# Layer one's running modulation parts: from TensorE rows to VectorE sums and TensorE columns

## The reference

```
mod   = silu(c)     @ w_mod[l] + b_mod[l]     # (6*1024); split into sh1, sc1, gt1, sh2, sc2, gt2
mod_c = silu(c_ctx) @ w_mod[l] + b_mod[l]
h = modulate(rms_norm(x, g_norm1[l]), sh1, sc1)
...                                            # attention, differential attention, convolution, merge
x = x + gt1 * y
h = modulate(rms_norm(x, g_norm2[l]), sh2, sc2)
x = x + gt2 * ((silu(h @ w_g) * (h @ w_u)) @ w_ffn_out)
```

## Time and profile before

| | |
|---|---|
| median of 3 runs | 2515.21 us (2509.43 to 2518.45) |
| span of the profiled execution | 2511.4 us, 34741 instructions |
| time of the profiled execution beyond its span | not shown apart; the median is 3.8 us above the span |
| PE busy, PEld busy | 2411.4 us (96%), 2171.6 us (86%) |
| DVE, ACT, POOL busy | 1223.0 us (49%), 1114.2 us (44%), 999.6 us (40%) |
| DMA | 209.07 MB, mean 83 GB/s |
| mean granted TensorE clock | 0.988 of 2.4 GHz |

### The profile page before, as it was taken

The page is one execution under the profiler, slowest core; times in us unless marked ns, Lnnn a source line. Parts: engine busy times, 40 slices in busy tenths (PEclk is TensorE's granted clock), DMA queues, the critical chain, the costliest instruction groups (busy, mean ns, idle before and its releaser), DMA issues.

```text
span 2511.4 us, 34741 instructions
## 1 busy us (share of the span) xinstructions
PE 2411.4 (96%) x13568; PEld 2171.6 (86%) x13568; DVE 1223.0 (49%) x1901; ACT 1114.2 (44%) x2219; POOL 999.6 (40%) x771
## 2 busy tenths in 40 slices
PE   7999999999989989999999998998999999999999
PEld 4888999889989989999999997777777877788887
DVE  5666677799943331111111126767878973311111
ACT  4666666542253253323322336656664253422222
POOL 2211122176555435555554542111224655444443
PEclk9999999999999999999999999999999999999999
DMA  6100111032223323333333322011112224233333
GB/s 247 43 26 26 34 43 43 18 103 86 75 94 118 121 65 112 118 107 112 114 107 98 118 71 89 26 43 34 43 40 70 93 87 137 81 99 99 95 97 96
DMA packets 117393, 209.07 MB, mean 83 GB/s; under 512 B 13680, under 2 KB 30320, under 8 KB 117104
## 3 DMA queue, kind: packets, MB, share of 16 engines
q1 hardware_dynamic: 117232, 206.86, 25.8%
HBM read 202.62 MB, written 4.19 MB: 82 GB/s over the span
## 4 chain that ended last, share of the span: by engine, by line
PE 51%; DVE 9%; ACT 3%; issue 2%; POOL 0%; DVEq 0%; ACTq 0%
PE acc L577 15%; PE acc L579 14%; PE acc L578 14%; DVE X L1674 4%; PE sco L699 2%; DVE RB L1551 1%; DVE M L1551 1%; ACT M L1006 1%; PE sco L749 1%; PE aux L762 1%; PE aux L577 1%; PE aux L578 1%; PE aux L579 1%; DVE NM L1594 1%; ACT RB L1006 1%
## 5 line engine op out<-in xcount | busy, mean ns | idle before, releaser
L499 POOL TENSOR_TENSOR WLO<-STG,WHI 128x512 fp32r<-128x512 f32 (+2 forms) x760 | 995.6, 1337 | 1493.4 <-ACT WHI L1002 1493.0
L577 PE MATMUL acc<-H,WHI 128*128 128x384 f32 (+2 forms) x1976 | 714.3, 361 | 19.7 <-DVE H L1780 12.1
L578 PE MATMUL acc<-H,WHI 128*128 128x384 f32 (+2 forms) x1976 | 696.4, 352 | 0.0
L579 PE MATMUL acc<-H,WLO 128*128 128x384 f32 (+2 forms) x1976 | 696.4, 352 | 0.0
L1002 ACT ACTIVATE WHI<-STG 128x512 fp32r<-128x512 f32 (+2 forms) x760 | 409.8, 591 | 488.9 <-PE acc L579 433.2
L577 PEld LDWEIGHTS acc<-H,WHI 128*128 128x128 f32 x1976 | 375.4, 190 | 49.2 <-issue 19.6
L579 PEld LDWEIGHTS acc<-H,WLO 128*128 128x128 f32 x1976 | 374.4, 189 | 25.7
L578 PEld LDWEIGHTS acc<-H,WHI 128*128 128x128 f32 x1976 | 375.6, 190 | 24.2
L1674 DVE SCALAR_TENSOR_TENSOR X<-U,WDW,X 128x783 f32<-128x783 f32 (+1 forms) x248 | 298.1, 1251 | 5.0 <-ACT X L1006 3.3
L577 PE MATMUL acc<-RB,WHI 128*128 128x384 f32 (+1 forms) x816 | 289.6, 355 | 5.8 <-DVE M L1551 5.4
L579 PE MATMUL acc<-RB,WLO 128*128 128x384 f32 (+1 forms) x816 | 287.7, 353 | 0.0
(11 more groups left out here) (134 smaller groups left out, 2924.8 us busy)
## 6 DMA issues: line engine op xcount, KB each, us to landing
STG<-in_w_fi SPq DMA_DIRECT2D x176, 256.0 KB, 2.9
STG<-in_w_mod SPq DMA_DIRECT2D x160, 256.0 KB, 2.7
STG<-in_w_in SPq DMA_DIRECT2D x104, 256.0 KB, 2.7
STG<-in_w_gate SPq DMA_DIRECT2D x96, 256.0 KB, 2.6
STG<-in_w_fo SPq DMA_DIRECT2D x64, 256.0 KB, 2.8
STG<-in_w_br SPq DMA_DIRECT2D x96, 128.0 KB, 2.1
FIRST<-in_w_mod SPq DMA_DIRECT2D x8, 1024.0 KB, 20.0
STG<-in_w_out SPq DMA_DIRECT2D x32, 256.0 KB, 2.9
```

The source lines that it names most:

```text
L499: nc.gpsimd.tensor_tensor(WLO[:, s, a:a + w], STG[:, g, a:a + w], WHI[:, s, a:a + w].bitcast(F32), ALU.subtract).then_inc(S("w_split"), 1)
L577: nc.tensor.matmul(dst, lh, rh, start=first, stop=False)
L578: nc.tensor.matmul(dst, lh, rl, start=False, stop=False)
L579: return nc.tensor.matmul(dst, ll, rh, start=False, stop=last)
```

## The change

The 56 mod tiles of layer 0's feed-forward leave the common list, and with them their `hi()`, `split`, `mod_half`, `mod_row`, `turn_mod` and `mod_group`. In their place:

- SP loads the same weights as 56 raw tiles of 512 KB (`raw`), 1 KB runs, into three slots of `M`: two after each up stage (none at stage 0 of group 0), one after each of the first 8 and 6 down tiles of groups 0 and 1. From the fourth on, each waits until DVE has used the raw tile three before.
- DVE weighs each raw tile (`weigh_raw`) after the stage's other work, in two instructions: for the first three parts both streams, 128 x 1024 each; for the last four the latent stream alone, in two halves of 128 x 512. Each adds to an accumulator `GV` in `M` or `U`.
- When eight raw tiles (one part) are in, PE sums over partitions (`turn_cols`): for each chunk of 128 channels and each stream one matmul with `GV` as the stationary operand and one column of ones as the moving one; 16 or 8 float32 matmuls, straight into columns of `sco`. DVE adds the bias (`col_sum`). Four parts are turned in the feed-forward, three around the norm between the layers.
- `U` is cleared on POOL after the third tile of layer 1, not on DVE in the merge of layer 0. The silu of c has a tile of its own, the context half of layer 1's `MOD` is cleared at the start, and PE's wait for the middle chunks stays at the first down tile only.

```diff
+LATER = [(0, GT2), (1, SH1), (1, SC1), (1, GT1), (1, SH2), (1, SC2), (1, GT2)]
+STREAMS = [2, 2, 2, 1, 1, 1, 1]
+RAWS = len(LATER) * KC
+RAW_UP = [[0, 2, 2, 2, 2, 2, 2, 2], [2] * 8, [2] * 6]
+RAW_DOWN = [[1] * 8, [1] * 6 + [0, 0], [0] * 8]
+TURN_UP = {(0, 6): 0, (1, 2): 2, (1, 6): 3}
+TURN_DOWN = {(0, 4): 1}
+RAW_SLOTS = 3
...
+        RAW = [M[:, D * i:D * (i + 1)] for i in range(RAW_SLOTS)]
+        GV = [[t[:, o + D * i:o + D * (i + 1)] for i in range(n)]
+              for (t, o), n in zip(((M, 3 * D), (U, 0), (M, 3 * D), (M, 5 * D), (U, 0), (U, D), (U, 2 * D)), STREAMS)]
...
+            def raw(i):
+                n, k = divmod(i, KC)
+                l, part = LATER[n]
+                g = l * MOD_GROUPS + part * 4
+                if i < RAW_SLOTS:
+                    sp.wait_ge(S("h_ready"), 2 * KC)
+                else:
+                    sp.wait_ge(S("gv"), 2 * (i - RAW_SLOTS + 1))
+                src = w_mod[g:g + 4, k // 4, :, k % 4 * MOD_GROUP:(k % 4 + 1) * MOD_GROUP].rearrange("g p c -> p g c")
+                sp.dma_start(RAW[i % RAW_SLOTS].rearrange("p (g c) -> p g c", g=4), src).then_inc(S(f"raw{i % RAW_SLOTS}"), 16)
...
                 for g, (k0, n) in enumerate(GROUPS):
                     for f in range(n):
                         for s in range(2):
-                            if mod_here(l, g, f):
-                                tile(w_mod[mods // 2, s], KC * P)
-                                mods += 1
                             tile(w_fi[l, f * 2 + (2 * k0 + s)], KC * P)
+                        for i in raws(l, "up", g, f):
+                            raw(i)
                     for j in range(KC):
-                        if mod_out(l, g, j):
-                            tile(w_mod[mods // 2, j % 2], KC * P)
-                            mods += 1
                         tile(w_fo[l, j][:, k0 * P:(k0 + n) * P], n * P)
+                        for i in raws(l, "down", g, j):
+                            raw(i)
...
+                    if l and t == 2:
+                        pool.wait_ge(S("col_full"), len(LATER))
+                        nc.gpsimd.memset(U[:, :], 0.0).then_inc(S("u_zero"), 1)
...
+            def turn_cols(n):
+                pe.wait_ge(S("gv"), 2 * KC * (n + 1))
+                if n >= 4:
+                    pe.wait_ge(S("col_sum"), n - 3)
+                for k in range(KC):
+                    for s in range(STREAMS[n]):
+                        mm = nc.tensor.matmul(turned_cols(n)[:, k, s:s + 1], GV[n][s][:, k * P:(k + 1) * P], ONES[:, 0:1],
+                                              start=True, stop=True)
+                mm.then_inc(S("col_full"), 1)
...
                 if l:
+                    turn_cols(4)
                     norm(l, 0, TOK)
+                    turn_cols(5)
+                    turn_cols(6)
...
+                        if l == 0 and (g, f) in TURN_UP:
+                            if g == 0:
+                                pe.wait_ge(S("mod_sum"), 1 + c.at("turn"))
+                            turn_cols(TURN_UP[g, f])
                         for s in range(2):
-                            if mod_here(l, g, f):
-                                mod_half(s)
-                            tile(KC, normed, slim, between=turn_pending if s == 0 else None)
+                            tile(KC, normed, slim)
...
+            def weigh_raw(i):
+                n, k = divmod(i, KC)
+                dve.wait_ge(S(f"raw{i % RAW_SLOTS}"), 16 * (i // RAW_SLOTS) + 16)
+                if k == 0 and n in (2, 4):
+                    dve.wait_ge(S("col_full"), n - 1 if n == 2 else 2)
+                w = RAW[i % RAW_SLOTS]
+                for u in range(2):
+                    if STREAMS[n] == 2:
+                        src, dst, gain = w, GV[n][u], SC[:, k, u:u + 1]
+                    else:
+                        src, dst, gain = w[:, 512 * u:512 * (u + 1)], GV[n][0][:, 512 * u:512 * (u + 1)], SC[:, k, 0:1]
+                    if k == 0:
+                        nc.vector.tensor_scalar(dst, src, gain, None, ALU.mult).then_inc(S("gv"), 1)
+                    else:
+                        dve.wait_ge(S("gv"), 2 * (i - 1) + u + 1)
+                        nc.vector.scalar_tensor_tensor(dst, src, gain, dst, ALU.mult, ALU.add).then_inc(S("gv"), 1)
...
-                if l == 0:
-                    dve.wait_ge(S("c_split"), CC * (l + 1))
-                    nc.vector.memset(U[:, :], 0.0).then_inc(S("u_zero"), 1)
...
+                        for i in raws(l, "up", g, f):
+                            weigh_raw(i)
+                        if l == 0 and (g, f) in TURN_UP:
+                            col_sum(TURN_UP[g, f])
```

More of the change, by code:

```diff
@@ L160, in weight_tiles @@
         for g, (_, n) in enumerate(GROUPS):
-            w += [KC * P] * ((4 * n - 2 * (g == 0)) if l == 0 else 2 * n)
-            for j in range(KC):
-                w += ([KC * P] if mod_out(l, g, j) else []) + [n * P]
+            w += [KC * P] * (2 * n) + [n * P] * KC
     return w
@@ L322, in qk_count, with raws, turned_cols @@
             return 13 * l + (2 + j if j < 4 else 5 + 2 * (j - 3))
-        def mod_here(l, g, f):
-            return l == 0 and (g or f) > 0
+        def raws(l, counts, g, i):
+            order = [(a, b) for a in range(len(GROUPS)) for b in [("up", f) for f in range(GROUPS[a][1])] + [("down", j) for j in range(KC)]]
+            table = {"up": RAW_UP, "down": RAW_DOWN}
+            done = sum(table[kind][a][b] for a, (kind, b) in order[:order.index((g, (counts, i)))])
+            return range(done, done + table[counts][g][i]) if l == 0 else range(0)
+        def turned_cols(n):
+            o = 512 * (n // 2 % 2)
+            return sco[n % 2][:, o:o + 2 * KC].rearrange("p (k s) -> p k s", s=2)
         def paired(l, j):
@@ L511, in _ @@
             for l in range(DEPTH):
-                for _ in range(26):
+                for t in range(26):
                     split(KC * P)
+                    if l and t == 2:
+                        pool.wait_ge(S("col_full"), len(LATER))
+                        nc.gpsimd.memset(U[:, :], 0.0).then_inc(S("u_zero"), 1)
                 for kind, _, _ in merge_order(l):
@@ L951, in _ @@
                             tile_pair(slim, slim, 2 * KC * l + KC, (l, "up", 0), (l, "up", 1))
-                            at["turned", l, "up", g, f] = c.at("turn")
                             continue
+                        if l == 0 and (g, f) in TURN_UP:
+                            if g == 0:
+                                pe.wait_ge(S("mod_sum"), 1 + c.at("turn"))
+                            turn_cols(TURN_UP[g, f])
                         for s in range(2):
-                            if mod_here(l, g, f):
-                                mod_half(s)
-                            tile(KC, normed, slim, between=turn_pending if s == 0 else None)
-                        at["turned", l, "up", g, f] = c.at("turn")
-                    if g == len(GROUPS) - 1:
-                        turn_pending()
-                    for j in range(KC):
[L962 to L966, removed]
+                            tile(KC, normed, slim)
+                    for j in range(KC):
+                        if l == 0 and (g, j) in TURN_DOWN:
+                            turn_cols(TURN_DOWN[g, j])
+                        tile(m, mid, slim, ready=("mid_chunks", 1 + FC * l + k0) if j == 0 else None)
         @block.scalar
@@ L1524, in _ @@
                         hi()
[L1525 to L1528, removed]
+                        if squares and j == 1:
+                            act.wait_ge(S("gv"), 2 * RAWS)
+                            act.wait_ge(S("col_full"), 4)
                         if squares and j:
@@ L1889, in _ @@
                 norm(l, 0, TOK)
+                if l:
+                    for i in (4, 5, 6):
+                        col_sum(i)
                 if l == 0:
@@ L2032, in _ @@
                             c.step(name)
+                        for i in raws(l, "up", g, f):
+                            weigh_raw(i)
+                        if l == 0 and (g, f) in TURN_UP:
+                            col_sum(TURN_UP[g, f])
+                    if g == 0:
+                        dve.wait_ge(S("col_sum"), 7 if l else 1)
                     for j in range(KC):
-                        mod_groups(at["turned", l, "down", g, j])
+                        if l == 0 and (g, j) in TURN_DOWN:
+                            col_sum(TURN_DOWN[g, j])
                         residual(l, j, slim, GT2)
+                        for i in raws(l, "down", g, j):
+                            weigh_raw(i)
                         if j and l < DEPTH - 1 and g == len(GROUPS) - 1:
```

33 lines of the change are left out of this document (14 added, 19 removed).

## The result

The median is 2522.11 us (2511.57 to 2527.94, 20 runs) against 2512.68 us of the kernel before (2508.11 to 2519.50, 20 runs). The ratio is 1.0031 with a 95% interval of 1.0021 to 1.0041: slower, by some 8 us, where the forecast was 2497.4 us. The profiled execution is one of the faster: it took 2516.45 us, with a span of 2514.6, at a granted clock of 0.982, while the median clock of the 20 runs is 0.979 (0.988 in the profiled execution of before).

The account below looks back on a forecast made before the run. PE, busy for 96% of the span, was taken to bound the kernel. The terms -64.1 - 1.3 + 14.6 + 28 + 5 = -17.8 us, from 2515.2, gave 2497.4 us, with a range of 2483 to 2509.

Parts of the forecast that it names:

- 28 groups leave PE: Layer 0's feed-forward: 28 groups of two modulation tiles and one turn, 2.29 us each, leave PE: 64.1 us less.
- wait behind the first pair: PE's 1.75 us wait behind the first pair, for POOL's split of the fourth tile, mostly goes: 1.3 us less.
- four turns: Feed-forward: 112 one-column load-and-matmul pairs at 0.12 us, plus 0.3 for entering and leaving each call: 14.6 us more.
- fifteen waits: PE waits at up stages for an accumulator held by late loads, 5 of 2.6 and 10 of 1.55 us: 28 more.
- half clock: Lower PE clock behind the five waits of 2.6 us, 0.6 of them dropping it: 5 us more (0 to 25).
- The late raw load: Up stages: raw load waits for DVE, delaying the product tile and ACT's Silu; accumulator free 10.9 us after PE's previous-stage end.
- the eighteen stages: Raw tile late at stages 2 to 7 of group 0, 1 to 7 of group 1, 1 to 5 of group 2.
- Its size: SP's queue: raw tile and both product halves, 1 MB, take 5.4 us to the last half, making PE wait 2.6 us.
- The clock: Behind PE's waits: a drop costs 1.7 us, 0.6 of five long waits drop, none behind 1.5 us: 5 us more.
- The late loads drop the clock: Rival, up stages: last half 0.8 us later, fifteen waits grow by 12 us, clock falls each time: 2530 us, chance 0.15.
- The loads are in time: Rival, up stages: the next product tile lands before about 7.3 us, nothing waits, -50.8 us: 2464 us, chance 0.15.
- POOL and DVE: Rival: POOL and DVE block each other at each first weighing, 15 x 1.04 = 15.6 us: 2513 us, chance 0.12.

Follow-up runs that it names:

- e7: The kernel of e1 with each turn of the feed-forward cut in two, four chunks before one tile and four before the next: 2465.9 us, ratio 0.9801.
- e9: The change with the turns before up stages (0,7), (1,3) and (1,7) in place of (0,6), (1,2) and (1,6): 2518.9 us, ratio 1.0013.
- e11: The change, with SP issuing an up stage's second product tile (from stage 2 on) only when ACT has rounded the first: 2501.8 us, ratio 0.9942.
- e3: The change with only half of each raw tile loaded, 256 KB in place of 512: 2512.5 us, ratio 0.9993.
- e5: The change with every weighing 512 columns wide, the other 512 channels left out for the first three parts: 2504.4 us, ratio 0.9954.
- e10: The change, its late loads included, with each turn of the feed-forward cut in two: 2515.4 us, ratio 1.0010.
- e1: The change with SP's second raw load of an up stage moved behind the next product tile: 2469.0 us, ratio 0.9808.
- e2: The change with ACT doing both Silus before both roundings in layer 0's up stages, SP's order kept: 2467.1 us, ratio 0.9807.
- e4: The kernel of e1 with the four column sums (turns) of the feed-forward made twice: 2491.2 us, ratio 0.9902.

## Why the prediction failed, by its own steps

| term | forecast, us | profiled execution, us |
|---|---|---|
| 28 groups leave PE | -64.1 | -64.1 |
| wait behind the first pair | -1.3 | -1.4 |
| four turns | +14.6 | +12.2 |
| fifteen waits | +28 | +38.0 |
| half clock | +5 | about +14.8 |
| leaving and entering at the waits | nothing | about +4.0 |
| sum | -17.8 | +3.5 (measured +3.1) |

The last two terms together are PE's busy time for the same instructions, 583.36 us after less 564.52 in e7, 18.8 us. The feed-forward of e7 has no half rate but that behind its first pair:

```profile
895.40:1462.60 567.20, 564.52 (x3280) 564.23 (x3281) 249.96 (x296) 142.37 (x256) 213.32 (x136) 0.99 0.35 114
```

The stretches at half rate are 29.7 us long in the change, so they cost 14.8. The other 4 us are the ends of the fifteen waits, some 0.27 us each: the last matmul ahead of a wait overlaps with none behind it (0.16), and the first step behind it is 0.28 us in place of 0.17, as here, where the clock did not fall:

```profile
942.59 0.44 PE L600 MATMUL acc<-H,WHI 128*128 128x384 f32 x1 [2.06 <-ACT G L1042]
942.88 0.34 PE L601 MATMUL acc<-H,WHI 128*128 128x384 f32 x1
943.05 0.34 PE L602 MATMUL acc<-H,WLO 128*128 128x384 f32 x1
```

- **What leaves PE: right.** From the first product (897.73) to turn 4 (1462.67), e7's feed-forward takes 564.9 us, 53.8 less than before. -64.1 - 1.4 + 12.0 for its turns is -53.5. That the 2.29 us of a group came from one step of the chain was enough.
- **The turns: right in kind, 2.4 us too dear.** 0.109 us a pair, next to the dense row of 0.116; entering and leaving is in it. That they are hidden between the layers held.
- **The late raw load: right in place, chain and number.** SP's wait on DVE, the eighteen stages, the three hidden by turns (e9), none in the down part, the weighing's 1.22 us from start to start against 1.28. In the stage shown, PE went on at 1006.20, 11.05 us behind t = 0 (995.15, 0.10 before DVE's T at 995.25); forecast 10.9.
- **Its size: one of the two steps that failed, 10 us.** "The raw tile and both halves are 1 MB: 3.3 + 2.1 = 5.4 us to the last half." It counted what is ahead of the last half in SP's list and not what SP, once let go, issues right behind it: 2 MB in 2.4 us. At (0,4) the raw load went out behind 974.70 + 2.44 = 977.1, and ACT could round the second half at 983.92 only, 6.8 us later (DVE, then ACT):

```profile
974.70 4.87 DVE L1797 SCALAR_TENSOR_TENSOR M<-M,SC 128x1024 f32<-128x1024 f32 x4
```

```profile
982.15 0.63 ACT L1038 ACTIVATE WHI<-STG 128x512 fp32r<-128x512 f32 x1 [7.96 <-DMA STG<-in_w_fi]
983.92 0.63 ACT L1038 ACTIVATE WHI<-STG 128x512 fp32r<-128x512 f32 x1 [1.14 <-DMA STG<-in_w_fi]
```

  With nothing behind it (e11) the last half is there 5.3 us after the release in the mean, and the waits are at and below the forecast. The Trainium skill (DMA: Bandwidth & Descriptors, "Queues, rings and completion order") says that each DMA engine takes descriptors in ring order, and also that a later one may finish its write before an earlier one. From the first half alone one would take it that later loads of the same queue cost an earlier one nothing. e11 shows that here they cost about 1.1 us.
- **The clock: the other step that failed, 10 us.** "For five waits of 2.6 us, 0.6 of them dropping", and none behind the short ones. One fall was priced about right (1.7 us; the nine in the change cost 14.8); their number was not. Counted over the change, e3, e5, e9 and e10: 26 of 33 waits above 2.6 us are followed by half clock, 6 of 15 between 1.9 and 2.6, 5 of 27 below. In the change there were eight above 2.6, not five, because the waits were longer, and six of those dropped, with one more of 2.06 us; and the turns, to which the forecast gave no clock at all, dropped it twice more. The median run has a lower clock still (0.979), and lies 5.7 us above the profiled one.
- **A term left out, 4 us.** The sum has nothing for leaving and entering at a wait, though it has 0.3 us for each turn.
- **The range.** Its lower end, 2483, is the sum of the least terms. Added up in the same way, the most terms (7.5 for the landing, 12.4 for the turns, 3 for the clock) give 2520 and not 2509; and the clock was let go to 8 us here, where its own paragraph has 25.
- **The rivals.** *The late loads drop the clock* was what came in kind: the waits 10 us longer where it had 12, the clock 15 us where it had 25.5, because it fell behind seven of the fifteen waits and not behind each; 2522 us where it gave 2530. It deserved more than 0.15, since its two parts feed each other: the same lateness lengthens the waits and moves them to where the clock falls. *The loads are in time* is not the change, but it is e1 and e2, at 2467 to 2469 us where it gave 2464. *POOL and DVE* did not happen where it counts: the weighings of an up stage take 4.87 or 2.73 us for four (more only in the last stage of all), and POOL was idle for 16.81 us. The rule of the Trainium skill behind it (SBUF — State Buffer, "SBUF: two separate sides") agrees with the down part, where POOL works: the second of two weighings of 1024 columns there takes 2.31 us against 1.28, off the path. The row is least, median and most, in ns:

```profile
L1797 DVE SCALAR_TENSOR_TENSOR M<-M,SC x42: 743/1277/2309, 935.3 to 1231.9; 128x1024 f32<-128x1024 f32 x28, 128x512 f32<-128x512 f32 x14
```

## What to carry to other kernels

When work leaves the bounding engine, follow each in-order queue that the new transfers pass: one load that waits for its buffer holds every load behind it, and an engine whose list has the rounding of that load ahead of a read of an accumulator hands the delay on. Moving either by one place was worth over 50 us here, three times what the change itself was forecast to bring (17.8). A released queue issued all that it held within 2.4 us here, so count the bytes behind the wanted load too. And price a wait of PE with the clock that it may cost and with its two ends: some 15 us here on top of 38 us of waits.

## What was not expected of the hardware

- Turns of 32 one-column pairs, 3.49 us with no idle time, were followed by 3 to 6 us at half the clock in 19 of 24 cases; cut in two with a product tile between, in none (12 halves of 16 pairs). In e4 the clock fell while the pairs were running. Why is not shown.
- A load in flight was slowed by about 1.1 us by loads issued behind it on the same queue, 1 MB more in the same 2.4 us (e11).
- A run's time follows its granted clock: of 20 runs of the change, three at 0.982 took 2514.6 us in the mean and seven at 0.978 took 2523.4. The median of one kernel and its profiled execution can differ by this alone. What sets the clock of a run apart from its twin's is not shown.
